# A two-block network in one kernel: the inverse's transposed copy made by turns, and the gated unit's sums over channels taken by VectorE

## The reference

```python
# RWKV-7 branch: 8 heads of 64, a state of 64x64 per head
def step(state, inp):
    r_t, w_t, k_t, v_t, kk_t, a_t = inp
    sa = jnp.einsum('bhvk,bhk->bhv', state, -kk_t)
    state = (state * w_t[:, :, None, :] + sa[..., None] * (kk_t * a_t)[:, :, None, :]
             + v_t[..., None] * k_t[:, :, None, :])
    y = jnp.einsum('bhvk,bhk->bhv', state, r_t)
    return state, y
...
# gated unit: normalisation over its 512 channels, then a causal mix of the tokens of a chunk
z = jax.nn.gelu(p, approximate=False)
u, v = jnp.split(z, 2, axis=-1)
mean = jnp.mean(vf, axis=-1, keepdims=True)
var = jnp.mean(jnp.square(vf - mean), axis=-1, keepdims=True)
v = ((vf - mean) * lax.rsqrt(var + EPS) * ln_g + ln_b).astype(p.dtype)
...
mixed = jnp.einsum('gij,bnjgd->bnigd', w, vc) + b_s.T[:, :, None]
return u * mixed.reshape(B, S, SG_WIDTH)
```

## Time and profile before

| | |
|---|---|
| median of 3 runs | 3377.36 us (3376.72 to 3378.01) |
| profiled execution, its own time | 3371.78 us |
| span of the profiled execution | 3369.9 us |
| TensorE busy | 3259.7 us, 97% |
| VectorE busy | 1919.7 us, 57% |
| ScalarE busy | 1449.1 us, 43% |
| GpSimd busy | 58.5 us, 2% |
| DMA moved | 357.91 MB, 106 GB/s on average |

### The profile page before, as it was taken

How to read it: one execution, slowest core, us unless ns; L and a number is a source line. 1 busy time by engine, 2 the same in 40 slices (tenths; PEclk the granted TensorE clock), 3 DMA queues, 4 the chain that set the end, 5 groups by cost and what they waited for, 6 DMA issues and landing times. The chain is left out here.

```text
span 3369.9 us, 53969 instructions
## 1 busy us (share of the span) xinstructions
PE 3259.7 (97%) x21844; PEld 2586.1 (77%) x21844; DVE 1919.7 (57%) x3313; ACT 1449.1 (43%) x2381; POOL 58.5 (2%) x44
## 2 busy tenths in 40 slices
PE   8999999999999999999999999999999999899998
PEld 6777788788877776787888888767678788566786
DVE  6555635677567446436775372358756642477555
ACT  6423523444245224434443243455643443655632
POOL 0010000000000110000000000000000000000000
PEclk9999999999999999999999999999999999999999
DMA  4223332232332214432223262212153342132342
GB/s 162 89 76 134 141 108 88 100 100 92 115 126 91 78 59 157 156 106 82 99 94 113 69 202 96 88 67 85 33 188 118 131 146 100 50 95 64 140 142 69
DMA packets 106822, 357.91 MB, mean 106 GB/s; under 512 B 12576, under 2 KB 12960, under 8 KB 103776
## 3 DMA queue, kind: packets, MB, share of 16 engines
q1 hardware_dynamic: 106592, 354.72, 31.3%
HBM read 309.98 MB, written 38.80 MB: 103 GB/s over the span
## 5 line engine op out<-in xcount | busy, mean ns | idle before, releaser
L224 PE MATMUL banks<-h_high,weights_high 128*128 128x512 f32 x2448 | 981.5, 401 | 23.0 <-DVE weights_low L245 15.7
L225 PE MATMUL banks<-h_low,weights_high 128*128 128x512 f32 x2448 | 957.5, 391 | 0.0
L226 PE MATMUL banks<-h_high,weights_low 128*128 128x512 f32 x2448 | 957.3, 391 | 0.0
L224 PEld LDWEIGHTS banks<-h_high,weights_high 128*128 128x128 f32 x2448 | 461.3, 188 | 136.5 <-DVE weights_low L245 17.4
L226 PEld LDWEIGHTS banks<-h_high,weights_low 128*128 128x128 f32 x2448 | 461.4, 188 | 98.4
L225 PEld LDWEIGHTS banks<-h_low,weights_high 128*128 128x128 f32 x2448 | 461.8, 189 | 93.3 <-issue 3.3
L217 DVE TENSOR_TENSOR weights_low<-ring,weights_high 128x1024 fp32r<-128x1024 f32 x131 | 163.4, 1248 | 295.7 <-ACT weights_high L212 294.4
L1822 DVE TENSOR_TENSOR weights_low<-ring,weights_high 128x1024 fp32r<-128x1024 f32 (+2 forms) x124 | 164.6, 1327 | 293.3 <-ACT weights_high L1768 293.2
L1768 ACT CAST weights_high<-ring 128x1024 fp32r<-128x1024 f32 (+2 forms) x124 | 140.6, 1134 | 437.4 <-PE banks L226 437.2
L212 ACT CAST weights_high<-ring 128x1024 fp32r<-128x1024 f32 x131 | 137.2, 1047 | 353.0 <-PE banks L226 348.6
L1966 ACT CAST weights_high<-ring 128x1024 fp32r<-128x1024 f32 (+1 forms) x116 | 132.6, 1143 | 321.7 <-PE banks L226 321.7
(11 more groups left out here) (467 smaller groups left out, 5008.7 us busy)
## 6 DMA issues: line engine op xcount, KB each, us to landing
ring<-in_in SPq DMA_DIRECT2D x136, 512.0 KB, 3.9
ring<-in_up SPq DMA_DIRECT2D x88, 512.0 KB, 3.3
ring<-in_gates SPq DMA_DIRECT2D x72, 512.0 KB, 3.9
x<-in_gates SPq DMA_DIRECT2D x58, 512.0 KB, 4.0
ring<-in_down SPq DMA_DIRECT2D x32, 704.0 KB, 4.1
ring<-in_out SPq DMA_DIRECT2D x32, 512.0 KB, 3.3
ring<-in_branch SPq DMA_DIRECT2D x16, 768.0 KB, 4.4
stored<-g_spill SPq DMA_DIRECT2D x16, 768.0 KB, 4.6
```

What stands on the lines that cost most here:

```text
L224: pe.matmul(bank, core.wh[:, half, w], high, start=start, stop=False)
L225: pe.matmul(bank, core.wh[:, half, w], low, start=False, stop=False)
L226: return pe.matmul(bank, core.wl[:, half, w], high, start=False, stop=stop)
```

## The change

In the inverse stage TensorE no longer computes the transposed inverse at each level. Behind `level_x` and the piece that follows it, `turn_inv` transposes the four 128x128 parts of `inv` into bank 2, and VectorE copies the bank to `inv_t` (`tensor_copy`), at each of the five levels. Only at level 5 does `level_inv_t` still run, into the same bank, and VectorE adds it. The copy of the transposed matrix from another half, which ScalarE made, and three VectorE operations in front of the levels go. A transpose of a 128x128 part swaps its off-diagonal quarters, so the items of `inv_t` lie in another order (`turned_slot`), and `level_x`, `level_inv`, `mix` and `u` go round the quarters in another order and into other banks; the last tiles of `mix` are added by two VectorE operations where there was one.

In the branch stage VectorE adds the gated unit's four tiles pairwise (1024, then 512 columns) and TensorE multiplies the one sum by ones; the same for the squares, which ScalarE makes. `square_and_gate(0)`, `square_and_gate(1)` and the bias product move to behind the second sum on VectorE; the weight split of `("scores", 1)` moves ahead of `norm_pair(3)`. The three last places for blocks hold 2, 2 and 8 in place of 4, 4 and 4. The last products for retention and the gated unit change their order.

```diff
+            def turn_inv():
+                for n in range(4):
+                    at = slice(n * P, (n + 1) * P)
+                    mm = pe.transpose(banks[2][:, at], b_flat[:, at], core.eye[:, :])
+                mm.then_inc(sems["invT_mm"], 1)
...
             def level_x(left):
-                for j, kind in items:
-                    for h in range(2):
-                        at = token_half(h, 2 * kind)
-                        mm = pe.matmul(banks[4 + kind][half(h), j * 64:(j + 1) * 64], left[at, 4 * kind + j, :], inv[at, 4 * kind + j, :],
-                                       start=True, stop=True)
+                for kind, cc in blocks_of:
+                    for i, rho in quadrants:
+                        j, at = item(cc, 2 * kind + i), (2 * kind + cc) * 64
+                        mm = pe.matmul(banks[4 + rho][half(i), at:at + 64], left[half(rho), j, :], inv[half(rho), j, :], start=True, stop=True)
...
             def level_inv_t(s):
-                for j in range(8):
-                    for h in range(2):
-                        mm = pe.matmul(banks[2][half(h), j * 64:(j + 1) * 64], xs[half(h), j, :], inv_t[s][half(h), j, :],
+                for kind, cc in blocks_of:
+                    for i, rho in quadrants:
+                        j = turned_slot(kind, cc, rho)
+                        mm = pe.matmul(banks[2][half(i), j * 64:(j + 1) * 64], xs[half(i), x_slot(kind, cc, rho), :], inv_t[s][half(i), j, :],
                                        start=True, stop=True)
...
+                    both = [(i, h) for h in range(2) for i in range(2)]
+                    for i, h in both:
+                        pe.matmul(banks[6 + h][half(i), 0:64], lw[half(h), i, t], state[half(h), i, :], start=True, stop=False)
...
                     level_x(level_t[(n - 1) % 2])
                     recur(sequel(g, l, 0))
+                    if l == 1:
+                        pe.wait_ge(sems["masked"], 3 * g + 3)
+                    turn_inv()
                     fill(("x", g, l))
                     pe.wait_ge(sems["x_out"], n)
-                    if n > 1:
-                        pe.wait_ge(sems["invT_out"], n - 1)
-                    if l == 1:
-                        pe.wait_ge(sems["init"], 2 * g + 2)
+                    pe.wait_ge(sems["invT_out"], TURNS * g + l)
                     if l < LEVELS:
                         level_inv(s)
-                    if l == 1:
-                        pe.wait_ge(sems["masked"], 3 * g + 3)
-                    level_inv_t(s)
+                    else:
+                        level_inv_t(s)
                     recur(sequel(g, l, 1))
                     fill(("inv", g, l))
...
                 for l in range(1, LEVELS + 1):
+                    dve.wait_ge(sems["invT_mm"], TURNS * g + l)
+                    dve.tensor_copy(inv_t[s], eight(banks[2][:, :])).then_inc(sems["invT_out"], 1)
                     recur(sequel(g, l, 0))
...
-            pe.wait_ge(sems["sg_activated"], 1)
             pe.wait_ge(sems["score_out"], 2 * NCH)
-            for m in range(4):
-                mm = pe.matmul(banks[2][:, :], core.ones[:, :], sg_v[:, m, :], start=(m == 0), stop=(m == 3))
-            mm.then_inc(sems["sg_mean_mm"], 1)
+            pe.wait_ge(sems["sg_summed"], 1)
+            pe.matmul(banks[2][:, :], core.ones[:, :], core.root[:, :], start=True, stop=True).then_inc(sems["sg_mean_mm"], 1)
...
+                if c == 0:
+                    act.wait_ge(sems["sg_centred"], 1)
+                    for k in range(2):
+                        act.activation(sg_squares[:, 2 * k:2 * k + 2, :], sg_v[:, 2 * k:2 * k + 2, :], ACT.Square)\
+                            .then_inc(sems["sg_squared"], 1)
...
+                if c == 3:
+                    extra_lows(dve, sems, core, e, ("scores", 1))
                 norm_pair(c)
+                if c == 2:
+                    dve.wait_ge(sems["sg_activated"], 1)
+                    own(dve.tensor_tensor(y[:, 0:2, :], sg_v[:, 0:2, :], sg_v[:, 2:4, :], ALU.add))
+                    own.settle()
+                    own(dve.tensor_tensor(core.root[:, :], y[:, 0, :], y[:, 1, :], ALU.add))
+                    own.tell(sems["sg_summed"])
...
-                 *((("y", c), (4, 4, 4, 0)[c]) for c in range(NCH)), ("turned", 4), ("sums", 4), ("mixed", 4)],
+                 *((("y", c), (4, 4, 4, 0)[c]) for c in range(NCH)), ("turned", 2), ("sums", 2), ("mixed", 8)],
```

More of the change, by code:

```diff
@@ L774, in recur @@
                         pe.wait_ge(sems["y_out"], 2 * c)
[L775 to L785, removed]
@@ new lines, in recur @@
+                    for i, h in both:
+                        j = item(cc, i)
+                        pe.matmul(banks[6 + h][half(i), 0:64], pq(s)[half(h), j, RCH:P], vt[half(h), j, :], start=False, stop=True)
+                    for i, h in both:
+                        pe.matmul(banks[6 + h][half(i), 64:P], lw[half(h), 2 + i, t], state[half(h), 2 + i, :], start=True, stop=True)
+                    for i, rho in both:
+                        j = item(cc, 2 + i)
+                        mm = pe.matmul(banks[6 + rho][half(i), P:P + 64], pq(s)[half(rho), j, RCH:P], vt[half(rho), j, :], start=True, stop=True)
@@ L790, in recur @@
                     mm.then_inc(sems["mix_mm"], 1)
                 if what == "u":
[L792 to L798, removed]
+                    pe.wait_ge(sems["mix_out"], 3 * c + 3)
@@ L799, in recur @@
+                    pe.wait_ge(sems["invT_out"], TURNS * (g + 1))
+                    for kind in range(2):
+                        for i, h in [(i, h) for h in range(2) for i in range(2)]:
+                            rho, at = row(h, kind), 256 + kind * 64
+                            mm = pe.matmul(banks[6 + i][half(rho), at:at + 64], inv_t[s][half(i), turned_slot(kind, cc, rho), :],
+                                           mix[half(i), 2 * kind + h, :], start=True, stop=True)
                     mm.then_inc(sems["u_mm"], 1)
@@ L979, in _ @@
                 steps(("tok", g))
-                act.wait_ge(sems["masked"], 3 * g + 1)
-                if g >= 2:
-                    act.wait_ge(sems["u_mm"], 2 * g - 2)
-                for h in range(2):
-                    act.copy(inv_t[g % 2][half(h), 4:8, :], neg_nt(g % 2)[half(1 - h), 4:8, :]).then_inc(sems["crossed"], 1)
                 steps(("pair", g))
@@ L1453, in _ @@
                 if c == 1:
-                    for m in range(4):
-                        pe.wait_ge(sems["sg_squared"], m + 1)
-                        mm = pe.matmul(banks[3][:, :], core.ones[:, :], sg_squares[:, m, :], start=(m == 0), stop=(m == 3))
-                    mm.then_inc(sems["sg_var_mm"], 1)
+                    pe.wait_ge(sems["sg_summed"], 2)
+                    pe.matmul(banks[3][:, :], core.ones[:, :], core.root[:, :], start=True, stop=True).then_inc(sems["sg_var_mm"], 1)
             pe.wait_ge(sems["sg_normed"], 4)
@@ L1637, in _ @@
             extra_lows(dve, sems, core, e, ("y", 3))
-            dve.wait_ge(sems["gated"], 1)
-            square_and_gate(0)
-            square_and_gate(1)
             dve.wait_ge(sems["sg_rooted"], 1)
```

83 lines of the change are left out of this document (45 added, 38 removed).

## The result

The median fell from 3377.04 to 3346.28 us (four runs each on one chip), -30.8 us; the ratio is 0.9911, interval 0.9894 to 0.9928. The change is faster, by 0.9%. I had said 3357.7 with a range of 3346 to 3367: right in sign, 11 us short in size, and the time lies 0.3 us inside the lower edge of the range. The profiled execution took 3347.93 us, 23.8 less than the one of before.

A forecast was written before the change was run, and what follows sets the result against it. TensorE, busy 3259.7 of 3369.9 us, was taken as the bound. Terms -29.1 + 18.0 - 2.7 + 4.1 - 10.6 + 0.6 = -19.7 us took 3377.4 to 3357.7, range 3346 to 3367.

The forecast's parts named there:

- `mix`: Inverse stage: its 16 products go round four quarters, 0.63 us instead of 0.80; -2.7 us in all.
- stops for VectorE: Inverse stage: TensorE waits 0.45 us at level 2 of groups 1 to 3, 0.7 at level 1 of group 3; +4.1.
- Products removed: Inverse stage, levels 1 to 4: `level_inv_t` goes 32 times at 0.91 us, gap staying, -29.1; level 5 gains nothing.
- The turn: Inverse stage, behind `level_x` at every level: four transposes cost 0.45 us, 40 times, +18.0 us.
- little start-up: Inverse stage, in each turn: a small addition to four transposes at 0.105 us, giving 0.45.
- Rival (c): New orders of `level_x`, `level_inv`, `mix` and `u` fall to the diagonal's rate: +38 us, 3396; chance 0.04.
- Rival (b): Inverse stage: copy, `level_inv`, addition, `level_x` become the bound; 0.5 us lost at 40 levels, +20, 3378; chance 0.10.
- these cover nearly every wait: Inverse and branch stages: blocks between small products cover waits; TensorE busy 180.65 of 183.00 and 88.02 of 93.00 us.
- Branch stage: Mean and variance keep one of four `ones` products each: 5.3 us less a layer, -10.6; a possible stop adds +0.6.
- the stop ahead of the transposes: Branch stage: TensorE asks for the normed tiles before VectorE has them; 0.3 us a layer, +0.6.
- End of the stage: Branch stage's end: VectorE's last chain runs beneath the last blocks, but the gate tile's transfer stays behind; 0 us.
- Rival (d): Both stages: gap goes with the removed products (-33.0), turns at 0.40, no stops; -30 us, 3347; chance 0.10.

The follow-up runs named there:

- first pair: The first profiled executions of the kernel before and the kernel after, with no further change: 3371.78 and 3347.93 us.
- the reordering experiment: Kernel after with `level_x` doing eight products on one diagonal, then eight on the other: 3357.45 us with two banks, 3361.07 with one.
- the branch stage alone: Kernel before with the branch function of after and its block places: median 3362.07 us, ratio 0.9955 to before.
- turn doubled: Kernel after with the four transposes of each turn issued twice into the same places: median 3367.02 us, ratio 0.9984.
- the inverse stage alone: Kernel after with the branch function of before: median 3356.92 us, ratio 0.9943 to before.
- repetition: Kernel after run once more, unchanged: median 3345.17 us, ratio 0.9909 to before.

## Why the prediction was right in its steps and short in its sum

The level-to-level distances make a full account of the inverse stages. In us over both layers:

| term | predicted | measured | how |
|---|---|---|---|
| levels 1 to 4: products out, turn in | -14.7 | -17.3 | 32 x (4.81 - 5.35) |
| level 5: turn in | +3.6 | +3.0 | 8 x 0.38 |
| `mix` | -2.7 | -3.0 | 10 x -0.17, up to a block, and 6 x -0.22, up to a turn |
| stops for VectorE | +4.1 | +5.0 | 6 x 0.55 and 2 x 0.83 |
| waits for nothing, gone | 0 | -2.7 | 1.06, 1.02 and 0.65 |
| sum | -9.7 | -15.0 | the stages: -8.2 and -6.8 in the first pair, -14.9 |

- **Products removed.** 0.91 foretold, 0.92 found (1.55 from `level_inv` to the block before, 0.63 after). The gap stayed, and level 5 gained nothing, as said.
- **The turn.** Mis-sized. I took 0.45, each costs 0.38 net (0.92 less 0.54): 2.8 us over 40. The added "little start-up" was not seen behind 64x64 products.
- **`mix`, `level_x`, `level_inv`, `u`.** Right. Rival (c) is refuted: the new orders run at 0.51 to 0.52, and the reordering experiment shows what the diagonal's rate would have looked like.
- **The stops.** Right in place, cause and roughly in size (0.55 and 0.83 for 0.45 and 0.7). Rival (b), the ring as the bound at each level, is refuted: the waits list has only these.
- **What I missed.** The step of the prediction that failed is "Both stages put blocks of big projections between the small products, and these cover nearly every wait": the 2.35 us between the stage's length and TensorE's busy time in the earlier trace rows were not taken apart. 1.7 of them were two waits for nothing. Had I listed the waits of the stage, I would have had a term with a size and no sign, since a change of the stream removes such waits (here), keeps them (the two of layer one with the branch stage alone) or makes one (turn doubled). They end with the late instruction transfers told above.
- **Branch stage.** The 5.3 a layer of the `ones` products is right: where the clock drops in both kernels, the stage of layer one fell from 93.3 to 88.05. By the mean of two executions each, the stages fell by 5.7 and 6.3, against the 5.0 of the sum. 0.3 of that is the stop ahead of the transposes that did not come. In layer two, first pair, neither stage had a drop at its start; TensorE's waits for the gate's staging tiles fell from 1.6 to 0.6 us, and those for a transfer from 0.7 to 0. With the branch stage alone the first is 1.6 still, with the inverse stage alone it is 1.0 in the layer without a drop and 0 in the other, so the change of the branch stage alone does not move it. What does is not shown.
- **End of the stage.** Worth nothing, as said, for the reason given: the gap is 4.4 before and after, with the transfer last in both. The new places are not quite idle, though: without them VectorE ends last in the new kernel, and 0.3 a layer is lost.

The sum of all stages is -27.4 by the means of the table; of the 7.7 missing from my sum 5.3 lie in the inverse stages, 1.9 in the branch stages, 0.5 between the layers. The medians say -31 to -32, with intervals that reach from -24 to -36. So -27.4 lies inside the interval. The last 4 us would be in the second block, where one execution differs from the next by more than that (2001.75 to 2010.64 over all kernels run here), and the granted clock goes with most of them. It is on record for 50 executions of before and 10 of after: a line fitted through each kernel's times, with one slope for both, gives 1.8 us for each 0.001 of mean clock, and -27.7 (interval 1.2 either way) between the kernels at the same clock. On the repetition's chip alone it gives -29.3, within 1.9. An estimate, but it meets the stages. Rival (d), at 3347, named the total that came, with turns at 0.40 (near the 0.38 found), no gap and no stops (both false): the total was near, the mechanism was not. In the prediction's chances, faster adds up to 0.87, not 0.86.

## What to carry to other kernels

Cost small products by the distance between starts and by the part of the array that neighbours in time use; 16 products on two quarters cost nearly two times those on four, whatever their banks. A transposed copy may then be cheaper to turn than to compute: four transposes for 0.38 in place of 16 diagonal products for 0.92. Where runs of a long kernel scatter by more than the effect, compare stage by stage between an engine's own starts: here a few tenths of a us could be told in a stage, where the median's interval is 10 us wide. Compare at like granted clock too. And list the waits of each stage that the change touches, those for nothing too, and look in the DMA records for an instruction transfer that ends just before them: they can vanish or appear with any change of the instruction stream.

## What the runs showed that I had not expected

- TensorE's waits that no semaphore and no engine explains stand at fixed instructions over repeated executions (0.9 and 1.0; 0.8 and 1.1) and move when the stream changes: none in the inverse stage after, one of 2.2 with 80 more transposes a layer. All nine end 1.25 to 1.47 us after a 16 KB transfer of instructions.
- A stop costs more than its bracket says: 0.36 of idle time is 0.55 between starts, since the bracket begins only at the last record's end, which is 0.2 behind its start.
- The halved rate of two quarters is not a matter of banks: 0.90 for `level_x` with one or two, 1.07 and 1.08 for `level_inv_t`.
- The untouched second block took from 2001.75 to 2010.64 us. In one stretch of the kernel after, 2800 to 2900 us, the granted clock was 0.93, and 0.98 in the same stretch of its repetition.
- A branch stage whose start falls into a drop of the clock keeps TensorE busy for 1.4 to 1.6 us more (88.0 and 86.7 before, 82.8 and 81.3 after), in either layer.
